# GLA layer of a hybrid decoder step: the scores of a token group's second and third chunk issued in one stretch, and the first token group prepared earlier

## The reference, cut to what matters

```python
def step(s, blk):
    qc, kc, vc, gc = blk
    b = jnp.cumsum(gc, axis=1)
    diff = b[:, :, None] - b[:, None, :]
    w = jnp.exp(jnp.where(causal[None, :, :, None, None], diff, -jnp.inf))
    scores = jnp.einsum('bihd,bjhd,bijhd->bhij', qc, kc, w)
    o = (jnp.einsum('bhij,bjhe->bihe', scores, vc)
         + jnp.einsum('bihd,bhde->bihe', qc * jnp.exp(b), s))
    b_last = b[:, -1]
    s = (s * jnp.exp(b_last)[..., None]
         + jnp.einsum('bjhd,bjhe->bhde', kc * jnp.exp(b_last[:, None] - b), vc))
    return s, o
```

## Time and profile before

| | us |
|---|---|
| median of three runs | 2381.43 |
| the profiled execution | 2380.08 |
| its span | 2378.0 |
| PE busy | 2357.6 |
| DVE busy | 1303.6 |
| POOL busy | 1224.1 |
| ACT busy | 792.7 |

### The profile page before, as it was taken

How to read it: one execution, slowest core, us unless ns; L and a number is a source line. 1 busy time by engine, 2 the same in 40 slices (tenths; PEclk the granted TensorE clock), 3 DMA queues, 4 the chain that set the end, 5 groups by cost and what they waited for, 6 DMA issues and landing times. The chain is left out here.

```text
span 2378.0 us, 45319 instructions
## 1 busy us (share of the span) xinstructions
PE 2357.6 (99%) x17808; PEld 2314.2 (97%) x17808; DVE 1303.6 (55%) x2038; ACT 792.7 (33%) x1253; POOL 1224.1 (51%) x1445
## 2 busy tenths in 40 slices
PE   9999999999999999999999999999999999999998
PEld 9999899999999999999989999999999999999997
DVE  6863353345545545566676776633444544545566
ACT  4701442222222222232454666522223223222224
POOL 2554146475665665676311212355566566666671
PEclk9999999999999999999999999999999999999999
DMA  4223031111111111113211111131111111111112
GB/s 164 65 65 91 28 131 45 45 45 45 54 45 45 54 44 46 54 36 113 70 46 66 55 48 66 55 122 45 45 45 45 48 52 45 46 54 45 45 55 83
DMA packets 41676, 142.48 MB, mean 60 GB/s; under 512 B 6448, under 2 KB 10160, under 8 KB 40336
## 3 DMA queue, kind: packets, MB, share of 16 engines
q1 hardware_dynamic: 32768, 106.78, 13.8%
q10 hardware_dynamic: 8720, 33.01, 4.0%
HBM read 120.42 MB, written 14.88 MB: 57 GB/s over the span
## 5 line engine op out<-in xcount | busy, mean ns | idle before, releaser
L749 PE MATMUL PS<-RB,WH 128*128 128x384 f32 (+1 forms) x4368 | 1081.6, 329 | 0.0
L749 PEld LDWEIGHTS PS<-RB,WH 128*128 128x128 f32 x4368 | 768.3, 188 | 5.8 <-issue 2.3
L749 PE MATMUL PS<-RA,WH 128*128 128x272 f32 (+2 forms) x3520 | 768.8, 308 | 2.8 <-DVE RA L1920 0.8
L749 PE MATMUL PS<-RB,WL 128*128 128x384 f32 (+1 forms) x2232 | 728.7, 326 | 0.0
L655 POOL TENSOR_TENSOR WH<-WR,FEW 128x256 fp32r<-128x256 f32 x420 | 325.6, 806 | 589.6 <-PE PS L749 560.7
L749 PEld LDWEIGHTS PS<-RA,WH 128*128 128x128 f32 x3520 | 585.9, 188 | 10.9 <-issue 4.1
L749 PE MATMUL PS<-RA,WL 128*128 128x272 f32 (+2 forms) x1760 | 540.5, 307 | 0.0
L749 PEld LDWEIGHTS PS<-RB,WL 128*128 128x128 f32 x2232 | 419.0, 188 | 0.0
L659 POOL TENSOR_TENSOR WL<-WR,WH 128x256 fp32r<-128x256 f32 x420 | 375.9, 925 | 0.0
L749 PEld LDWEIGHTS PS<-RA,WL 128*128 128x128 f32 x1760 | 330.7, 188 | 0.0
L2021 DVE TENSOR_TENSOR X<-PS,X 128x544 f32<-128x544 f32 x280 | 202.6, 724 | 204.2 <-PE PS L749 204.2
(11 more groups left out here) (238 smaller groups left out, 2255.7 us busy)
## 6 DMA issues: line engine op xcount, KB each, us to landing
WR<-ws SPq DMA_DIRECT2D x189, 512.0 KB, 3.5
EB<-xT ACTq DMA_DIRECT2D x8, 544.0 KB, 5.7
x_spill<-X ACTq DMA_DIRECT2D x8, 544.0 KB, 2.7
EB<-x_spill ACTq DMA_DIRECT2D x8, 544.0 KB, 6.6
GA<-st_gla ACTq DMA_DIRECT2D x4, 1024.0 KB, 4.8
glas_o<-GA ACTq DMA_DIRECT2D x4, 1024.0 KB, 3.9
yT<-X SPq DMA_DIRECT2D x16, 208.0 KB, 1.9
X<-xT ACTq DMA_DIRECT2D x4, 544.0 KB, 6.0
```

Source lines behind the costliest of these rows:

```text
L749: return nc.tensor.matmul(out, lhsT, rhs, start=start, stop=stop, skip_group_check=True)
```

## The change

The PE part of item `A2` gets an item of its own, `A2P`. DVE's part (the masks) stays at `A2`. In the loop, `A2P` of the next place is issued when that place is the first of its token group; when it is the second, `A2P` of the second and of the third place are issued one after the other, in banks 3 and 4 or 4 and 3; when it is the third, none is issued, since it is done already. Nothing is removed or added in instructions. PE's third stretch so moves ahead of: the second half projection of that turn, `B` of the first place, the halves behind it, `GNM`, `A` of the third place, and the half behind that. Its wait, for the mask of the token group's first place, moves with it. ACT and DVE have no part in `A2P`.

Before the loop the items of the first token group are put earlier: `SPA(0, 0)` after the first `L`, `SPD(0, 0)` after the second, turn 0 of `prepare(0)` before the last group of k, turn 1 from there to the second group of v, and turn 2 before v's second unit; and turn 0 of `prepare(1)` stands before `L(1, 0)` rather than after v's second unit. PE's own order before the loop stays the same. ACT's copy of the weights for v's second unit (at the first item of v) now has the softplus of groups 1 and 2 and the exponentials of turns 0 and 1 ahead of it.

```diff
     low, q0, k0, v0, v1 = (S(u) for u in UNITS[:5])
-    s = low + q0[:1] + [("GL",)] + q0[1:] + k0[:1] + [("L", 0, 0), ("L", 0, 1)] + k0[1:2] + [("SPA", 0, 0, 1), ("L", 0, 2)]
-    s += k0[2:] + [("SPD", 0, 0, 1), ("SPA", 0, 1, 3)] + v0[:1]
     first = [part for turn in range(3) for part in prepare(0, turn)]
-    s += first[0] + first[1] + v0[1:2] + first[2] + [("SPD", 0, 1, 3)] + v0[2:] + first[3] + v1[:1] + first[4]
-    s += [("L", 1, 0), ("L", 1, 1)] + v1[1:2] + first[5]
-    s += [("A", 0, 0), ("A2", 0, 0), ("L", 1, 2)] + v1[2:] + prepare(1, 0)[0] + prepare(1, 0)[1] + [("SPA", 1, 0, 1)]
+    s = low + q0[:1] + [("GL",)] + q0[1:] + k0[:1] + [("L", 0, 0), ("SPA", 0, 0, 1), ("L", 0, 1), ("SPD", 0, 0, 1)] + k0[1:2]
+    s += [("L", 0, 2)] + first[0] + first[1] + k0[2:] + [("SPA", 0, 1, 3)] + first[2] + v0[:1] + [("SPD", 0, 1, 3)]
+    s += first[3] + v0[1:2] + first[4] + v0[2:] + first[5] + v1[:1] + prepare(1, 0)[0] + prepare(1, 0)[1]
+    s += [("L", 1, 0), ("L", 1, 1)] + v1[1:2]
+    s += [("A", 0, 0), ("A2P", 0, 0), ("A2", 0, 0), ("L", 1, 2)] + v1[2:] + [("SPA", 1, 0, 1)]
...
                 s += (take(1) if p == 8 else []) + [("A",) + PLACES[k + 1]] + take(1)
+                if (p + 1) % 3 != 2:
+                    s.append(("A2P",) + PLACES[k + 1])
+                if (p + 1) % 3 == 1:
+                    s.append(("A2P",) + PLACES[k + 2])
                 s.append(("A2",) + PLACES[k + 1])
...
-                elif kind == "A2":
+                elif kind == "A2P":
                     h, c = item[1:]
                     if place(h, c) > 1:
```

## The result

| | us |
|---|---|
| kernel before, median of 18 runs | 2381.86 (2380.11 to 2384.15) |
| changed kernel, median of 18 runs | 2386.48 (2382.21 to 2388.53) |
| ratio, 95% interval | 1.0017 [1.0011, 1.0024] |
| changed kernel, profiled execution | 2388.44, span 2386.4, granted clock 0.995 |

I had forecast 2380.9 us and a range up to 2384.0. The two profiled executions differ by 8.4 us, the medians by 4.6: that of the kernel before is one of its fastest, that of the changed kernel one of its slowest. The runs of the changed kernel follow the granted clock: 2382.2 us at 0.999, 2384.4 to 2386.7 at 0.997, 2388.4 to 2388.5 at 0.995. Those of before do so too: of 27 runs timed beside the first four experiments those at 0.999 took 2379.6 to 2381.0 us and those at 0.997 took 2382.6 to 2383.9.

What follows compares the result with a forecast made beforehand. PE, busy 99% of the span, was taken as the bound, with only its waits and junctions to win. Terms summed to -0.55 us on the profiled 2380.08; with the median 1.35 above that execution, 2380.9 us, range 2376.8 to 2384.0.

Steps and rivals of the forecast that it cites:

- part 4: Before the loop: DVE's instructions move to where it idles, so place 0's wait goes, -1.33 us; bounds -1.33 and 0.
- e = 1: Pair before preparation 1 (e numbers the preparation whose first stretch follows the pair): -1.35 us, bounds +0.58 and -1.80.
- e = 2: Pair before preparation 2: GNM already waits for DVE, so 0.27 of the 0.58 disappears in that wait; +0.31 us.
- e = 3: Pair before preparation 3: junction gain 0.30, and the stretch fills the wait for ACT's copy, another 0.28.
- e = 9: Pair before preparation 9: the last level has more room than the 0.88 us needed, so a gain of 0.30.
- e = 10, 11: Pairs before preparations 10 and 11: 10 is late already, +0.58 us; 11 has 0.18 to spare, +0.40.
- last pair: Places 34 and 35: no preparation comes after it, so the junction's gain stays, -0.30 us.
- e = 3, 6 and 9 have room: Preparations 3, 6 and 9: 2.4 us of room against 0.88, gain 0.30 each; with ACT's copy wait filled, -1.18 us together.
- Junction 0.30: PE's time lost entering and leaving a score stretch: one junction goes per merged pair, 0.21 to 0.31 us, taken as 0.30.
- stretch 0.58: PE's third stretch ahead of GNM delays its chain by 0.58 us; +0.58 each at preparations 4, 5, 7, 8, 10.
- Part 3: Preparation 1: POOL's move shortens DVE's chain by 1.95 us against 0.58 added, leaving 0.45 of place 3's wait; -1.35 us.
- plain work put in front of the chains: Rival: junctions don't shrink, eight chained pairs cost 0.69 each, no relief or 1.33; +5.5, 2386.9 us; chance 0.08 with similar.

Runs made afterwards that it cites:

- the first four experiments: e1 to e4, four kernels that each take parts of the change, run together beside the kernel before, which had a median of 2382.06 us there.
- e12: e11 with pairs only in the third token group of heads 0 to 2, and head 2's samples' matmuls split by a half projection: 2373.00 us, ratio 0.9960.
- e7: Kernel before, without any part of the change, with each matmul of the samples' CO items issued twice: 2405.38 us, ratio 1.0095.
- e9: Changed kernel with half projections spread among the samples' small matmuls in heads 0 and 2, one half kept before head 0's GNM: 2380.13 us, ratio 0.9993.
- e4: Kernel before with the new order before the loop and pairs only in token group 2 of every head: 2379.74 us, ratio 0.9992.
- e3: Kernel before with the new order before the loop and pairs only in token groups 0 and 1 of every head: 2382.22 us, ratio 1.0003.
- e6: Changed kernel with GNM one half projection earlier at the first place of the second token group in heads 1 and 2: 2382.73 us.
- e10: e9 with GNM one half projection earlier at the first place of the second token group of heads 1 and 2: 2376.95 us, ratio 0.9980.
- e11: As e10, with the new order before the loop, but without pairs and without the split of CO in head 2: 2373.26 us, ratio 0.9965.
- e1: Kernel before with only the new order before the loop, scores in the loop issued as before: 2379.95 us, ratio 0.9993.
- e2: Kernel before with only the loop's pairs, the preparation before the loop being the old one: 2391.08 us, ratio 1.0042.

## Why the prediction was wrong

Here is how far the changed kernel falls behind or gets ahead in each stretch, in us: differences of the two profiled executions, by the starts of the transposes of each place, against the terms:

| stretch | predicted | measured |
|---|---|---|
| place 0 (part 4) | -1.33 | -1.32 |
| e = 1 | -1.35 | -1.41 |
| e = 2 | +0.31 | +0.28 |
| **e = 3, head 0's samples** | **-0.58** | **+2.64** |
| e = 4 | +0.58 | +0.58 |
| e = 5 | +0.58 | +0.77 |
| e = 6 | -0.30 | -0.23 |
| e = 7, 8 | +0.58 each | +0.58, +0.57 |
| **e = 9, head 2's samples** | **-0.30** | **+3.98** |
| e = 10, 11 | +0.58, +0.40 | +0.58, +0.49 |
| **last pair to the end** | **-0.30** | **+0.79** |

Against -0.55 the profiled executions differ by +8.4; of the 8.9 between them 7.5 are the terms of e = 3 and e = 9, and 1.1 is the last pair. The changed kernel's profiled execution has both falls of the clock; its one run at 0.999 took 2382.2 us, which lies inside my range, but 1.2 us or more above before at that clock and not 0.55 below.

1. **The step that failed** is "e = 3, 6 and 9 have room [...] Gain 0.30 each". The room in the chain is there, and the gain is real once nothing else happens (e12: -0.28, -0.27). But the sum treated small matmuls as work that TensorE can always have at 8 to 12 ns each. In heads 0 and 2 the pair stands in front of `CO`, TensorE reaches the end of its instructions and stands for 1.4 and 1.1 us, and runs at 1.2 GHz for 6.9 us behind it. e7 shows the mechanism without the change, and e9 takes it away from the change: 2386.48 - 2380.13 = 6.35 us, and with an estimate of 0.9 for three more junctions 7.3 us. The range had no term for either, since I read the clock as one number, 0.999, and not by stretches, and passed over the stand of 1.17 us in the earlier trace rows's view, where it is a row of its own:

```profile
PE PS L749 <- issue: 1.2, 1, 1.2
```

2. **The last pair** was costed with "has no preparation after it". Something else is after it: PE's output of place 34 and all that hangs on it reach DVE later, and the MLP's first matmuls wait for DVE's low part, 1.1 us in place of 0.2. e4, with pairs in the third groups alone, has the same wait of 1.1, and e3, without them, 0.2. Which of the instructions in between carries the delay I did not trace.

3. **Junction 0.30 and stretch 0.58** held at e = 2, 4, 7, 8 and 10 within 0.04 us, and e6 shows that the chain starts at `GNM`. e = 5 and e = 11 came 0.19 and 0.09 dearer, for which I have no cause. At e = 5 and 8 I had the place of the wait wrong: it is the read of bank 7 that grows, not the first stretch. All pairs together were forecast at about +2.4 us; e10 against e11 gives 3.4, but there two of the chains are no longer as late, so that the agreement with 2.4 + 1.1 for the last pair is in part luck.

4. **Part 3 and part 4** held to 0.06 us. Both were forecast together with a pair; alone, in e1, they give 2.6 us from place 0 to place 4 of the profiled executions, and about 2 us of the whole at equal clock (2377.9 to 2378.1 at 0.999, where before had 2379.6 to 2381.0).

5. **The rival that came nearest in time**, plain work put in front of the chains, 2386.9, was wrong in each of its parts: the junctions shrank, e = 1 got its relief, the 1.33 came.

That e9's 2380.13 lies 0.8 us below the forecast does not save it: the kernel before has a stand of its own, which e9 has not, and by the clock of 0.997 in many of its runs it has a fall as well (no trace of such a run was taken).

Open: which stands bring the clock down. In the traces of this study all thirteen falls in the GLA part begin inside a stand beside the samples' matmuls or within 1.7 us of its end. Four stands there, of 0.66 to 1.44 us, had none, among them that of the kernel before. Waits of up to 1.3 us between large matmuls had none either. So a stand there was needed for a fall in every trace, but was not enough, and its length alone does not decide.

## What to carry to other kernels

A run of hundreds of small matmuls has a price that no engine's busy time shows: it can outrun its own instructions, and the stand can be followed by several us at half of TensorE's clock. Before putting two such runs together, look at the issue rows of the list of waits, at the granted clock by stretches and at the packets of the instruction queue; between two runs put a few us of large matmuls, and don't take them from where they cover another wait. Work moved ahead of an item that starts another engine's chain costs its whole length wherever that chain ends late (0.57 to 0.77 us, at five of twelve places here); moving the item itself forward was worth 1.6 to 1.9 us a place, where merging gives 0.30.

## What the runs showed of the hardware

- Instructions come in packets of 16 KB, about 126 matmuls with their weight loads. In all sixteen stands for issue of the GLA part, over eight kernels' traces, TensorE went on 2.2 to 2.75 us after a packet's start.
- `CO` matmuls of 128 x 8 run 8.5 ns apart, so a packet can be used up in 1.1 us, by this estimate (126 x 8.5 ns); a score stretch runs at 12 ns apiece.
- A stand of 0.76 us beside small matmuls was followed by 1.2 GHz (e3), one of 1.44 us in another kernel was not (e2's profiled execution). Half clock lasted 3.4 or 6.8 us in the GLA part.
- The spread of a kernel's times told of it: 6.3 us in the changed kernel, 0.5 to 1.4 in the four whose traces have no fall in the GLA part (e9 to e12). A fall that comes in some executions only is easily missed in one trace.
